# Expert lists and load order in the mixture-of-experts end of a decoder step on one Trainium2 core

## The reference, cut to what matters

```
logits = einsum('nd,de->ne', t, w_router);  probs = softmax(logits);  sel = probs + b_router
grp_score = top_k(sel.reshape(n, 4, 4), 2)[0].sum(-1);  best = argmax(grp_score)
_, idx = top_k(where(in_grp(best), sel, -inf), 2)
w = p_sel / sum(p_sel);  gates = sum(one_hot(idx) * w)
act = silu(t @ wg[e]) * (t @ wu[e]) * gates[e]        # wg, wu: 1024 x 512 per expert
moe = sum over e of act @ wd[e]                       # wd: 512 x 1024 per expert
y = x + gate * moe
```

## Time and profile before

| | |
|---|---|
| median of 3 runs | 1250.47 us (1250.44 to 1253.88) |
| the profiled execution, its own time | 1251.76 us |
| its span, first to last instruction | 1250.0 us |
| mean granted clock of PE | 0.977 |
| PE busy | 1157.8 us, 93% of the span |
| DVE busy | 617.3 us, 49% |
| ACT busy | 338.4 us, 27% |
| POOL busy | 247.7 us, 20% |
| loads issued: gate, up, down | 39, 37, 37 |

### The profile page before, as it was taken

One profiled execution on the slowest core, in us unless ns is written; L12 is line 12 of the kernel. 1 busy time (PEld: TensorE's weight loads), 2 busy tenths in 40 slices (PEclk: granted clock), 3 DMA queues, 4 the chain that ended last, 5 costly groups with the idle time before them and its releaser, 6 DMA issues.

```text
span 1250.0 us, 19133 instructions
## 1 busy us (share of the span) xinstructions
PE 1157.8 (93%) x6692; PEld 545.1 (44%) x6692; DVE 617.3 (49%) x1246; ACT 338.4 (27%) x716; POOL 247.7 (20%) x303
## 2 busy tenths in 40 slices
PE   6999999999989999898999989999999999998872
PEld 4444444444446666565444444433333333333230
DVE  0010867777689989997855649322112121112110
ACT  2132222122048888787121221000000000000000
POOL 2011110111059400000100011222322322222221
PEclk8999999999989999999999989999999999999987
DMA  9933333322267465447233284658946499979994
GB/s 359 338 126 101 103 101 105 122 88 73 72 191 242 143 226 185 138 136 270 73 113 101 68 314 135 245 197 283 334 144 234 127 333 397 347 260 376 397 394 163
DMA packets 116180, 254.96 MB, mean 204 GB/s; under 512 B 14478, under 2 KB 28942, under 8 KB 115080
## 3 DMA queue, kind: packets, MB, share of 16 engines
q1 hardware_dynamic: 95425, 211.04, 48.1%
q0 software_dynamic: 16704, 38.30, 8.9%
q10 hardware_dynamic: 3984, 4.72, 1.1%
HBM read 370.93 MB, written 38.17 MB: 327 GB/s over the span
## 4 chain that ended last, share of the span: by engine, by line
PE 76%; DMA 11%; DVE 4%; ACT 4%; issue 4%; SPq 1%; POOL 0%; ACTq 0%; POOLq 0%; DVEq 0%
PE bank L1584 20%; PE bank L1987 17%; PE bank L2001 7%; PE bank L1775 6%; DMA big<-in_w_up_dram 5%; PE bank L1564 3%; PE bank L1618 2%; PE bank L1658 2%; DMA big<-in_w_gate_dram 2%; DMA big<-in_w_down_dram 2%; PE bank L1668 2%; PE bank L1646 2%; PE bank L1876 2%; PE bank L1439 1%; PE bank L1978 1%
## 5 line engine op out<-in xcount | busy, mean ns | idle before, releaser
L1987 PE MATMUL bank<-big,mid 128*64 128x512 f32 x1120 | 257.2, 607 | 17.4 <-DMA big<-in_w_up_dram 8.5
L1584 PE MATMUL bank<-big 128*128 128x512 f32 x560 | 249.2, 598 | 0.1
L1584 PEld LDWEIGHTS bank<-big 128*128 128x128 f32 x560 | 103.6, 190 | 131.3 <-issue 131.3
L2162 DVE SCALAR_TENSOR_TENSOR cvT<-low,cw,cvT 128x256 f32<-128x256 f32 x360 | 156.9, 509 | 0.0
L1987 PEld LDWEIGHTS bank<-big,mid 128*64 128x64 f32 x1120 | 79.9, 139 | 167.9 <-issue 165.6
L2001 PE MATMUL bank<-big,mid 128*64 128x512 f32 x544 | 119.7, 592 | 2.5 <-DMA big<-in_w_down_dram 2.5
L2267 DVE TENSOR_TENSOR_SCAN big<-big 128x513 f32<-128x513 f32 (+4 forms) x96 | 90.1, 977 | 9.0 <-ACT big L1187 9.0
L2849 DVE TENSOR_TENSOR xt<-xt,bank 128x512 f32<-128x512 f32 x18 | 12.4, 687 | 139.1 <-ACT xt L1381 129.0
L878 POOL TENSOR_TENSOR st<-st,mhalf 128x16 f32<-128x16 f32 (+1 forms) x9 | 25.2, 2801 | 252.6 <-DVE st L2193 243.8
L2001 PEld LDWEIGHTS bank<-big,mid 128*64 128x64 f32 x544 | 39.8, 137 | 79.9 <-issue 79.9
L2868 DVE TENSOR_TENSOR mid<-bank,low 128x512 f32<-128x512 f32 x34 | 21.9, 685 | 105.5 <-PE bank L2001 71.6
(11 more groups left out here) (450 smaller groups left out, 1384.2 us busy)
## 6 DMA issues: line engine op xcount, KB each, us to landing
big<-in_w_gate_dram SPq DMA_DIRECT2D x39, 2048.0 KB
big<-in_w_up_dram SPq DMA_DIRECT2D x37, 2048.0 KB, 18.3
big<-in_w_down_dram SPq DMA_DIRECT2D x37, 2048.0 KB, 22.7
low<-in_w_ada_dram SPq DMA_DIRECT2D x32, 512.0 KB, 4.1
low<-in_cache_v_dram SPq DMA_DIRECT2D x64, 256.0 KB
big<-in_w_in_dram SPq DMA_DIRECT2D x8, 1280.0 KB, 17.3
xt<-in_x_prompt_dram SPq DMA_DIRECT2D x16, 512.0 KB, 4.7
mid<-in_w_ada_dram SPq DMA_DIRECT2D x8, 1024.0 KB, 14.2
```

Source lines behind the costliest of these rows:

```text
L1584: mm = pe.matmul(bank[:, 4 if cc == 2 else cc, :], hT[:, s, k, :], w_in_sb[:, k, cc * 512:(cc + 1) * 512], start=(k == 0), stop=(k == KD - 1))
L1987: mm = pe.matmul(bank[half, 2 * s + w, :], xgT[:, s, k, half], w_sb[:, x, k, :], start=(k == 0), stop=(k == KD - 1))
L2162: c.put(V.scalar_tensor_tensor(out, src, cw[:, ch, tap:tap + 1], out, ALU.mult, ALU.add))
```

## The change

It has four parts. In `load_early_expert` SP issues the gate matrix as before, and then waits for both gathers of early rows before it issues the up and the down matrix. In `expert_order` the groups are taken in cyclic order from the early expert's group, and within every group the experts in cyclic order from the early expert's place in its group. The unit numbers of both lists are limited to the last unit of their half (`r_au`, `r_bu`). The DVE instructions that prepare this are added, and some of the old order's are gone. The description of the change also speaks of logits of a tile one iteration later; no line of the diff moves them.

```diff
@@ buffers
+        e_parts_i = sb("e_parts_i", [P, 2, E], I32)
+        e_parts = sb("e_parts", [P, 2, E])
+        r_au = small(MT)
@@ load_early_expert (SP)
-                for w_sb, w_d, landed in zip((wg_sb, wu_sb, wd_sb), (w_gate, w_up, w_down), e_w_in):
+                for w, (w_sb, w_d, landed) in enumerate(zip((wg_sb, wu_sb, wd_sb), (w_gate, w_up, w_down), e_w_in)):
+                    if w == 1:
+                        for arrived in xg_in:
+                            sp.wait_ge(arrived, EARLY)
@@ DVE, ahead of the loop over the tiles
+            c.put(V.tensor_scalar(e_parts_i[:, 0, :], row_no_i[:, 0:E], EPG.bit_length() - 1, None, ALU.arith_shift_right))
+            c.put(V.tensor_scalar(e_parts_i[:, 1, :], row_no_i[:, 0:E], EPG - 1, None, ALU.bitwise_and))
+            c.wait()
+            c.put(V.tensor_copy(e_parts[:, :, :], e_parts_i[:, :, :]))
@@ expert_order (DVE)
-                op(V.tensor_reduce(b_grp, b_exp.rearrange("p (g j) -> p g j", g=EG), AX_X, ALU.add))
-                op(V.scalar_tensor_tensor(b_key, b_exp, -float(E), expert_no, ALU.mult, ALU.add))
-                op(V.scalar_tensor_tensor(b_key.rearrange("p (g j) -> p g j", g=EG),
-                                          b_grp.unsqueeze(2).broadcast_to([P, EG, EPG]), -4.0 * E,
-                                          b_key.rearrange("p (g j) -> p g j", g=EG), ALU.mult, ALU.add))
-                op(V.tensor_tensor(x_before[:, :, :], row(b_key, E, E), b_key.unsqueeze(2).broadcast_to([P, E, E]), ALU.is_lt))
-                op(V.tensor_reduce(b_place, x_before[:, :, :], AX_X, ALU.add))
+                op(V.tensor_tensor(b_two, e_parts[:, :, :], row(b_exp, 2, E), ALU.mult))
+                op(V.tensor_reduce(b_own_parts, b_two, AX_X, ALU.add))
+                op(V.tensor_tensor(b_two, e_parts[:, :, :], b_own_parts.unsqueeze(2).broadcast_to([P, 2, E]), ALU.subtract))
+                op(V.tensor_scalar(b_wrap, b_two, 0.0, float(EPG), ALU.is_lt, ALU.mult))
+                op(V.tensor_tensor(b_two, b_two, b_wrap, ALU.add))
+                op(V.scalar_tensor_tensor(b_place, b_two[:, 0, :], float(EPG), b_two[:, 1, :], ALU.mult, ALU.add))
+                c.put(V.tensor_tensor(x_before[:, :, :], row(b_place, E, E), b_place.unsqueeze(2).broadcast_to([P, E, E]),
+                                      ALU.is_lt))
@@ experts_of (DVE)
-                for x, unit in ((0, unit_no), (1, r_bu)):
+                for x, unit in ((0, r_au), (1, r_bu)):
@@ ahead of the first list (DVE)
-            c.put(V.tensor_scalar(r_bu, unit_no[:, 0:MB], r_cut, None, ALU.add))
+            c.put(V.tensor_scalar(r_gm, units, -1.0, None, ALU.add))
+            c.put(V.tensor_scalar(r_half, r_cut, -1.0, None, ALU.add))
+            c.wait()
+            c.put(V.tensor_scalar(r_bu, unit_no[:, 0:MB], r_cut, r_gm, ALU.add, ALU.min))
+            c.put(V.tensor_scalar(r_au, unit_no[:, 0:MT], r_half, None, ALU.min))
```

More of the change, by code:

```diff
@@ L327, in decoder_step @@
         b_top, b_top_rank, b_used = early(1), early(1), early(1)
-        b_exp, b_key, b_grp, b_place = early(E), early(E), early(EG), early(E)
-        b_next = b_at32.rearrange("p a n -> p (a n)")[:, 0:E * E].rearrange("p (e j) -> p e j", e=E)
+        b_exp, b_key, b_place = early(E), early(E), early(E)
+        b_room = b_at32.rearrange("p a n -> p (a n)")
+        b_next = b_room[:, 0:E * E].rearrange("p (e j) -> p e j", e=E)
+        b_two, b_wrap = (b_room[:, E * E + 2 * E * j:E * E + 2 * E * (j + 1)].rearrange("p (w e) -> p w e", w=2) for j in range(2))
+        b_own_parts = b_room[:, E * E + 4 * E:E * E + 4 * E + 2]
         assert EB0[0] <= 17416
```

## The result

The kernel after takes 1237.39 us (median of 13 runs, 1235.1 to 1248.26), the kernel before 1250.47 in the same comparison: a ratio of 0.9899, with a 95% interval of 0.988 to 0.9918. The gain is 13 us where 32 were forecast, and the time lies above the range of 1209 to 1231. The profiled execution's own time is 1239.8 us (span 1238.0), against 1251.76 for the one that is shown of before: 12.0 less.

The account below looks back on a forecast made before the run. PE, 93% busy, was taken to share the passes with a full DMA. Passes −20.1, last pass −16.7 and SP's wait +4.5 sum to −32.3: 1219.5 from the profiled 1251.76, 1218 as median, range 1209 to 1231.

Parts of the forecast that it names:

- rival 1: Passes with one new expert in a row saturate the DMA flow, each of 12 losing 1.1 us: 1231; chance 0.12.
- rival 3: Slower: every pass with one new expert loses 3.1 us, 12 of them 37: 1255; chance 0.03.
- Rival 2: SP's wait ahead of the early up and down matrices costs nothing: 1213; chance 0.12.
- Rival 4: The order on the chip differs from the one worked out and only the clamp acts, −10.9: 1240; chance 0.03.
- The first gate load ... 0, at most 3: Gate load for pass 1, before the passes: its 2.10 MB and a pass's fetches fit, costing 0, at most 3 us.
- The bare double cost 6.0, and I take 7 (5 to 10): Pass 12, the one pass left with two new experts: costs 7 us, where pass 4 lost 6.0 before.
- I take +4.5: SP's wait delays tile 6's h2 store and tile 8's work: 3 us of lateness plus 1.5 of low clock.
- DVE ends at +19.9: Last pass: DVE finishes 19.9 us after pass 16's end, waiting for POOL's fetch, where before it took 36.6.
- 15.1 from pass 16's end: Last pass: PE's own work in pass 17 was sized at 15.1 us, letting DVE end at +16.6.
- tail −16.7: Last pass: clamp and one down load instead of two save 16.7 us (12.5 to 18.7) up to DVE's end.
- −27.1 for the losses that went: Up to pass 16: three passes with two new experts go, with what follows them, saving 27.1 us.
- the list of one-load passes in the signs: Sign of being right: SP's pairs take the one-load time at passes 1, 2, 3, 5, 8, 11, 14 to 17.

Follow-up runs that it names:

- experiment 9: Kernel after without SP's wait, experts' places fixed in a spread order with no double and no new expert in pass 1: 1218.38 us.
- experiment 5: Kernel after, SP's wait kept, with the stores of x1 and h2 of tile 6 issued ahead of that wait: 1232.2 us.
- experiment 10: Kernel after without SP's wait, with the early expert's group fixed as 15 14 13 12, so no double at pass 12: 1217.65 us.
- experiment 1: Kernel after without SP's wait ahead of the early up and down matrices; order and clamps stay: 1230.26 us.
- experiment 2: Kernel before with SP's wait alone added: 1257.51 us.
- experiment 8: Kernel after with POOL waiting for the gate matrices of pass 1 before issuing the fetches and gathers of passes 0 to 3: 1240.25 us.
- experiment 4: Kernel before with the cyclic order alone, without clamp or SP's wait: 1236.03 us.
- experiment 6: Kernel after without SP's wait, with the stores of tile 6 ahead of the early up and down matrices: 1231.4 us.
- experiment 7: Kernel after, SP's wait kept, with the early expert's group fixed as 15 14 13 12, so no double at pass 12: 1226.54 us.
- experiment 11: As experiment 10, with POOL waiting for the gate matrix of pass 1 ahead of the third tile's gather of h2 rows: 1217.08 us.
- experiment 12: As experiment 1, with sampled output rows fetched to a spare tile and not added, so POOL skips waiting for them before the next fetch: 1226.7 us.
- experiment 16: As experiment 1, with the gather of gate rows issued early in each step, ahead of POOL's wait for the combine: 1229.26 us.
- experiment 14: As experiment 9, with the gather of gate rows issued ahead of POOL's wait for the scatter of the sampled rows: 1231.77 us.
- experiment 15: As experiment 9, with the gather of gate rows issued early in each step, ahead of POOL's wait for the combine: 1219.63 us.

## Why the prediction was wrong

What held: the direction; the lists to the pass, with 12 singles and the double of pass 12 (14 new experts); the skipped pair of gates; that the h2 store, and not the gather, decides how late pass 0 starts; that the last combine waits for a fetch; that singles in a row cost no wait for a matrix (0.6 us in all here, none in experiment 9), so that rivals 1 and 3 fail. Where singles follow each other the chain of fetches can still cost something, as in the profiled executions of experiments 5 and 10 (4.5 and 8.8 us at passes 3 and 4). Rival 2 falls with experiments 1 and 2. Rival 4 gives nearly the measured time and is wrong all the same: the order on the chip is the one worked out. That its 1240 is near is luck. The miss is in the sizes of four terms, 19.8 of 20.4 us in the profiled execution.

- **"The first gate load ... 0, at most 3" (the term that was most wrong): 7.9 measured.** The load is issued at 805.31 and PE wants it at 812.94, 7.6 us later; it lands at 817.44. PE waits 4.64 us, and its next product takes 6.65 instead of 3.65. The prediction counted bytes, 2.10 MB and "a pass's fetches", which fit. It did not look at when they run: the first transfers of POOL, five of them (two fetches of output rows, a gather of gate rows, two of h2 rows), are issued from 804.93 to 814.41, in the very stretch of the load:
```profile
804.93 1.05 POOL L988 DMA_INDIRECT low<-out_dram,o_col  x1 [0.92 <-POOL o_col L982]
...
814.41 0.97 POOL L977 DMA_INDIRECT mid<-h_d,x_col  x1 [0.80 <-POOL x_col L974]
```
Before, no new expert came in pass 1, so no row showed a load there. Experiment 8 divides the term: by PE's timeline, with POOL's transfers held back the first step takes 30.8 us, not 37.3, where it takes 29.4 without a load. So 1.4 us is the load's own, as it takes 8.16 us even alone and not the 5.4 of its bytes at 385 GB/s, and the rest comes from what runs beside it. The 7.9 is at the high end: in the nine other profiled kernels with this load and POOL's transfers beside it (experiments 1, 4 to 7, 10 to 12 and 16) the first step loses 3.1 to 8.8 us, all of them more than the 1.4 of experiment 8. The Trainium skill ("DMA: Bandwidth & Descriptors", section Queues, rings and completion order) says that each DMA engine takes packets in turn from the queues that have work. The trace fits that, with 11.69 us for the load against 8.16 alone, but shows no single packets.
- **"The bare double cost 6.0, and I take 7 (5 to 10)": 11.5 measured, 10.9 by experiment 7.** It was sized by pass 4, which has a quiet pass ahead (pass 3 takes no new expert). Pass 12 has the singles of passes 10 and 11 ahead, and it loses in two places, gate and up; that these singles took away the lead of its loads is the likely reason, and no run takes them away to show it. The prediction named both singles and gave them 1 us.
- **"I take +4.5" for SP's wait: 7.6 in the profiles, 7.1 and 7.3 by experiments 1 and 2.** The mechanism was right and the store's landing too (749.4, forecast 746 to 749.5); the value was taken from the middle of that range and it came at its end, +3.5 and not +3, with a colder stretch behind it: the early gate stretch takes 12.90 us where it took 10.57, +2.3 instead of 1.5, and 1 us more in small operations between. Some 0.7 of the 7.6 were there before the wait. The gather did come earlier, and PE multiplied the early rows from 734.35 instead of 737.12, but the store was waited for all the same, so nothing came of it; what it would bring without the late store no run shows.
- **"DVE ends at +19.9": +24.2.** What is late is the fetch, as forecast, but the prediction priced it from a pass in the quiet middle. There the scatter is issued 3.7 us behind the pass's end and the last fetch 7.8 behind the scatter. At the end the combine of pass 16 is itself late by its own fetch (DVE idles 8.48 us for it), so the scatter comes 6.4 us behind the pass's end, and the last fetch 10.7 behind the scatter. The combines before are late too: from that of pass 13 on, a turn of the chain takes 26.6, 22.8 and 21.2 us against PE's 22.5. In the other profiled kernels with both fetches and one new down matrix in the last pass the end takes 24.7 to 27.0, so 24.2 is the low end. PE's own work was sized too small as well: "15.1 from pass 16's end" leaves out the 3.45 us that PE idles ahead of its first product of pass 17, 3.49 in the kernel after. With them it is 18.6, which experiment 1 shows (18.5, from 1196.96 to 1215.48), and DVE could not end before some +20 whatever the fetch did. In experiment 12, where DVE waits for PE alone, it ends at +21.6.
- The edits on DVE cost nothing, as forecast, though the constants took 2.6 us (1.23, 0.16 and 1.24) and not under 1.

The terms, forecast and measured: wait +4.5 and +7.6; first gate 0 and +7.9; double +7 and +11.5; other singles 0 and +0.6; tail −16.7 and −12.4. With −27.1 for the losses that went, that is −32.3 and −11.9. Two readings of the rows are off without moving the sum: two of the last eight slices before, not one, lie under 333 GB/s (260 and 163), and the list of one-load passes in the signs leaves out passes 4 and 10. The step that failed, in one sentence: each transfer was weighed by its bytes against a mean flow, and not by what was queued beside it when it ran; for the first gate load this took a term at 0 that measured 7.9. Experiment 10, which avoids the double and leaves SP's wait out, gives the 1218 that the whole change was forecast to give; that is a coincidence, as it lacks two of the forecast's own costs.

What stays open: which of POOL's transfers delays the first gate load (experiment 11 moves only the two that are issued last, and hardly changes what runs beside the load), and why the loss there varies from 3.1 to 8.8 us between profiled executions; why clamp and order together bring less than their sum, if they do; what an earlier gather would bring; and what sets the 4.0 to 8.7 us of the second fetch, since by experiments 14 and 15 its neighbour in POOL's queue is at most part of it. Experiments 9, 10, 11 and 15 take 1217 to 1220 with nothing left out, but with an order written for these inputs; of those that work the order out, experiments 1 and 16 are the best, at 1230 and 1229, and the noise does not tell them apart.

## What to carry to other kernels

Price a new load by the stretch in which it is in flight, with everything that the other queues issue there, not by a pass's bytes. When loads have been taken off the path, look at the next loop-carried chain, here the scatter and the fetches of the output's rows, over its whole length and not only in the last pass: a turn of it took 21 to 27 us where PE's pass takes 22.5. And before adding the gains of two edits, measure them together: clamp and order gave 13.4 and 14.2 alone and 19.9 together.

## What the hardware showed beyond that

- Indirect fetches of output rows took 4.6 us from issue to landing around the early rows. In the passes (the turns on the chains of the kernel after and of experiment 9) the first fetch took 2.3 to 6.7, the second 4.0 to 8.7, and a scatter 3.4 to 7.9. In the stretches where the chain bound, it was the sum of the three, not the engines' work, that made the loop's period.
- The first gate load, 2.1 MB, took 8.16 us with no row transfers beside it and 9.84 to 12.71 with them.
- A 0.5 MB store that stood behind two matrices in SP's queue landed 15.1 us after its issue (kernel after); where the same store stood ahead of them (experiment 5), PE turned tile 8 at 745.50 without a wait.
- Of the three small operations that make the order's constants, two took 1.23 and 1.24 us (16 and 32 elements), the one between them 0.16. Why is not shown.
